# Feed-forward scales: a row of 256 values through DRAM in place of a product on TensorE

## The reference, cut to what matters

```
y = x * rsqrt(mean(x * x) + eps)          # one scale per token
x = x + s * (silu((y * g) @ w_gate) * ((y * g) @ w_up)) @ w_down     # s is 0.5 or 1.0
```

## Time and profile before

| what | value |
|---|---|
| median of 3 runs | 1790.29 us (1788.45 to 1790.33) |
| the profiled execution, its own time | 1788.07 us |
| its span in the trace | 1786.4 us |
| TensorE, weight loads, VectorE, ScalarE, GpSimd busy | 99%, 83%, 69%, 55%, 13% |
| TensorE's granted clock | 1.00 |
| mean DMA rate | 177 GB/s |

### The profile page before, as it was taken

One profiled execution on the slowest core, in us unless ns is written; L12 is line 12 of the kernel. 1 busy time (PEld: TensorE's weight loads), 2 busy tenths in 40 slices (PEclk: granted clock), 3 DMA queues, 4 the chain that ended last, 5 costly groups with the idle time before them and its releaser, 6 DMA issues.

```text
span 1786.4 us, 25450 instructions
## 1 busy us (share of the span) xinstructions
PE 1773.3 (99%) x9448; PEld 1479.0 (83%) x9448; DVE 1231.7 (69%) x1753; ACT 988.0 (55%) x1333; POOL 226.2 (13%) x255
## 2 busy tenths in 40 slices
PE   9999999999999999999999999999999999999999
PEld 8888877888888888877888877778888877788887
DVE  6775667677557755767776489976775599867763
ACT  6554586565445554666555476555554466645551
POOL 0000131000000000320000096200001383100000
PEclk9999999999999999999999999999999999999999
DMA  8756472555546564544665563535656544545651
GB/s 266 221 195 203 138 211 73 188 188 188 212 145 195 194 224 143 190 119 143 195 197 198 166 212 124 181 128 182 201 195 207 168 162 143 188 159 173 192 202 75
DMA packets 221517, 316.26 MB, mean 177 GB/s; under 512 B 14168, under 2 KB 162288, under 8 KB 221168
## 3 DMA queue, kind: packets, MB, share of 16 engines
q1 hardware_dynamic: 221392, 315.02, 54.1%
q10 hardware_dynamic: 32, 0.01, 0.0%
HBM read 313.94 MB, written 1.05 MB: 176 GB/s over the span
## 4 chain that ended last, share of the span: by engine, by line
PE 84%; DVE 9%; DVEq 3%; ACT 2%; issue 1%; ACTq 0%; POOL 0%; POOLq 0%
PE ps L2091 25%; PE ps L1955 14%; PE ps L1957 13%; PE ps L1956 13%; PE ps L2092 13%; DVE w_lo L1222 3%; PE ps L1965 1%; ACT w_hi L717 1%; PE ps L2206 1%; PE ps L2179 1%; DVEq L1706 1%; PE ps L2194 1%; DVEq L1742 1%; DVE score L1731 1%; DVE att L1755 1%
## 5 line engine op out<-in xcount | busy, mean ns | idle before, releaser
L1222 DVE TENSOR_TENSOR w_lo<-raw,w_hi 128x2048 fp32r<-128x2048 f32 (+2 forms) x296 | 674.5, 2301 | 200.9 <-ACT w_hi L717 199.2
L2091 PE MATMUL ps<-aT,w_hi 128*128 128x512 f32 x1920 | 667.9, 392 | 0.0
L717 ACT ACTIVATE w_hi<-raw 128x2048 fp32r<-128x2048 f32 (+2 forms) x296 | 551.5, 1891 | 158.9 <-PE ps L1957 155.7
L2092 PE MATMUL ps<-aT,w_lo 128*128 128x256 f32 x1920 | 537.7, 280 | 0.0
L2091 PEld LDWEIGHTS ps<-aT,w_hi 128*128 128x128 f32 x1920 | 359.2, 187 | 79.8 <-issue 0.3
L2092 PEld LDWEIGHTS ps<-aT,w_lo 128*128 128x128 f32 x1920 | 362.9, 189 | 0.2
L1955 PE MATMUL ps<-w_hi,aT 128*128 128x512 f32 (+2 forms) x768 | 309.3, 403 | 4.3 <-DVE w_lo L1222 2.8
L1957 PE MATMUL ps<-w_hi,aT 128*128 128x512 f32 (+2 forms) x768 | 295.1, 384 | 0.0
L1956 PE MATMUL ps<-w_lo,aT 128*128 128x512 f32 (+2 forms) x768 | 294.2, 383 | 0.0
L1955 PE MATMUL ps<-w_hi,gT_hi 128*128 128x512 f32 x528 | 206.0, 390 | 0.0
L1957 PE MATMUL ps<-w_hi,gT_lo 128*128 128x512 f32 x528 | 205.6, 389 | 0.0
(11 more groups left out here) (289 smaller groups left out, 1704.0 us busy)
## 6 DMA issues: line engine op xcount, KB each, us to landing
raw<-in_w_in SPq DMA_DIRECT2D x120, 512.0 KB, 4.6
raw<-in_w_ffn_down SPq DMA_DIRECT2D x88, 512.0 KB, 4.4
raw<-in_w_ffn_in SPq DMA_DIRECT2D x88, 512.0 KB, 5.0
raw<-in_w_ffn_gate SPq DMA_DIRECT2D x86, 512.0 KB, 4.1
raw<-in_w_ffn_up SPq DMA_DIRECT2D x86, 512.0 KB, 5.1
raw<-in_w_ffn_out SPq DMA_DIRECT2D x44, 512.0 KB, 4.7
raw<-in_w_out SPq DMA_DIRECT2D x32, 512.0 KB, 4.7
raw<-in_w_ck SPq DMA_DIRECT2D x8, 512.0 KB, 3.9
```

What stands on the lines that cost most here:

```text
L717: nc.scalar.activation(dst, src, ACT.Copy).then_inc(units_hi, 1)
L1222: V.tensor_tensor(o, a, h, ALU.subtract).then_inc(units_split, 1)
L2091: M(o, wh, aT[:, :, k, :], start=k == 0, stop=False, skip_group_check=True)
L2092: r = M(o[:, 0], wl, aT_hi[:, k, :], start=False, stop=k == KC - 1, skip_group_check=True)
```

## The change

The row of scales no longer comes from TensorE. After the square root and the reciprocal, ScalarE's queue writes the 256 scales to a scratch in DRAM (one element per descriptor, since `rstd` holds one value per partition and column), waits until they have landed, and issues a second transfer that reads the 1 KB back twice into each of the 128 partitions. Only then does ScalarE go on to the silu of tile 0. VectorE waits for the second transfer where it waited for TensorE and copied. The diagonals, the product with ones, the two copies, and the `ones` tile with its fill on GpSimd are gone.

```diff
@@ allocations
-        ones = sb("ones", [P, P])
-        rstd_diag = att[:, 2048:2304]
+        scale_rows = nc.dram_tensor("scale_rows", (3 * DEPTH, SEQ), F32, kind="Internal").ap()
@@ gpsimd
-            nc.gpsimd.memset(ones[:, :], 1.0)
@@ scalar, ffn
                 def first_tile():
                     root(N)
+                    act.dma_start(scale_rows[F].rearrange("(i p) -> p i", p=P), rstd[:, 0:2],
+                                  allow_slow_non_contiguous=True).then_inc(row_written, 16)
+                    act.wait_ge(row_written, (F + 1) * 16)
+                    act.dma_start(rstd_row.rearrange("p (c n) -> p c n", c=2),
+                                  scale_rows[F:F + 1, :].unsqueeze(1).broadcast_to([P, 2, SEQ])).then_inc(row_loaded, 16)
                     act.wait_ge(units_used, st.used(p0 + 1))
@@ vector, ffn
                     if isinstance(t, int) and t == 1:
-                        dve.wait_ge(row_T, F + 1)
-                        V.tensor_copy(rstd_row[:, 0:SEQ], ps[:, 4, 0:SEQ])
-                        V.tensor_copy(rstd_row[:, SEQ:2 * SEQ], ps[:, 4, 0:SEQ])
+                        dve.wait_ge(row_loaded, (F + 1) * 16)
...
                     norm(N)
-                    for i in range(2):
-                        o = V.tensor_scalar(rstd_diag[:, P * i:P * i + P], ident[:, :], rstd[:, i:i + 1], None, ALU.mult)
-                    o.then_inc(diag_ready, 1)
@@ tensor, ffn
                 turned_tile(1, p0 + 2)
-                pe.wait_ge(diag_ready, F + 1)
-                M(ps[:, 4, 0:SEQ], ones[:, :], rstd_diag, start=True, stop=True).then_inc(row_T, 1)
```

More of the change, by code:

```diff
@@ L261, in build @@
         up_lo = sem("up_lo")
-        diag_ready = sem("diag_ready")
-        row_T = sem("row_T")
+        row_written = sem("row_written")
+        row_loaded = sem("row_loaded")
         gate_scaled = sem("gate_scaled")
```

## The result

The changed kernel takes 1826.74 us (median of 6 runs, 1824.92 to 1834.14) against 1788.49 us for the kernel before beside it (1788.10 to 1790.33): ratio 1.0217, 95% interval 1.0206 to 1.0227. The prediction was 1790.8 us, 0.86 on no change and 1788.0 to 1794.5 as its range: it was wrong. Span against span it is 1825.5 - 1786.4 = 39.1 us more.

The account below looks back on a forecast made before the run. The prediction took TensorE's stream as the bound. Removing the product gains 2.6 us and a stall in the first feed-forward loses 3.1: +0.5 us on the median 1790.29 gives 1790.8 us, range 1788.0 to 1794.5.

Parts of the forecast that it names:

- L: Time from issue to landing of ScalarE's write of the scales; taken as 3.5 us, with 2.0 as lower bound.
- upper bound: Longest landing allowed for the scales' write: 8.0 us, from a weight load close by in the first feed-forward.
- a stop costs no more than its length: TensorE's stall at tile 2 was counted only as its standing time: 2.9 us plus 0.15 in the first feed-forward.
- The mechanism of the wait: ScalarE's wait delays silu and splits: 4.1 us in the first feed-forward; 2.7 in the others, hidden up to L = 6.0.
- Rival (b): TensorE stops in all six feed-forwards, from L = 6.0 on; at 8.0, +15 us, 1805 us; chance 0.04.
- +2.5: Upper end in us, like -1.0 below, to which the range added about a microsecond for the spread of runs.
- All stops together: TensorE stands at tile 2 in the first feed-forward only, 3.1 us lost; the other five hide their delay.
- The product's 0.43 us a feed-forward: Removing TensorE's product with ones moves transposes and tile 2 up by 0.43 us, 2.6 us over six feed-forwards.
- Rival (d): Handover between tile 1 and transposes fills the gap, so TensorE gains nothing; first feed-forward loses 2.7, 1793.0 us; chance 0.05.
- Rival (e): TensorE's clock falls to half rate after the stop, losing 1.8 us: +2.3, 1792.6 us; chance 0.05.
- SyncE's later loads: Loads of the next units leave later when splits free slots late; 4.1 us in the first feed-forward reach no one.
- The read: The 256 KB read back arrives before VectorE asks, at 37.3 against 38.2 us in the first feed-forward; costs nothing.

Follow-up runs that it names:

- e2: Changed kernel, but the write is two rows of 512 bytes from the identity matrix instead of the scales; 1791.83 us, ratio 1.0021.
- e6: Kernel before without diagonals, product and copies, nothing in their place; tiles 1 to 10 are multiplied by values of `x`; 1787.95 us, ratio 0.9990.
- e12: Changed kernel, but the 256 single elements are written 64 bytes apart and the row is read from an input; 1792.31 us, one run.
- e4: Changed kernel with spare transposes into an unused bank where TensorE would stand, 48 and 20 in the first feed-forward, 5 and 20 in the others; 1823.93 us, ratio 1.0204.
- e11: Changed kernel with TensorE's wait for tile 2's unit moved ahead of the transposes and filled with 60 or 25 spare transposes; 1819.44 us, ratio 1.0169.
- e7: Changed kernel, but ScalarE waits for the write and issues the read only after silu and both splits; VectorE waits at the row's use; 1799.67 us, ratio 1.0062.
- e8: Changed kernel with both transfers issued from GpSimd's queue, so ScalarE never waits and VectorE waits at the row's use; 1809.99 us, ratio 1.0120.
- e1: Changed kernel, but the same 1 KB is written as 128 runs of 8 bytes, in another order of tokens; 1796.2 us, one run.
- e3: Changed kernel, but the 256 single elements are written 512 bytes apart and the row is read from an input; 1797.0 us, one run.
- e9: Changed kernel, but the first feed-forward keeps the product; the other five write 8-byte runs and VectorE reads with matching stride; 1788.44 us, ratio 0.9996.
- e5: Kernel before, product kept, with only the write of the scales and ScalarE's wait for it added; 1810.01 us, ratio 1.0114.
- e13_late_9: Kernel before with nine extra copies on ScalarE behind the square root of each of the last five feed-forwards, no transfer; 1818.88 us, one run.
- e13_late_11: Kernel before with eleven extra copies on ScalarE behind the square root of each of the last five feed-forwards, no transfer; 1829.51 us, ratio 1.0219.
- e10: Changed kernel with TensorE's wait for tile 2's first unit moved ahead of the transposes, without spare transposes; 1827.71 us, ratio 1.0218.

## Why the prediction was wrong

**The step that failed is the size of L.** It was taken as 3.5 us, with 8.0 as its upper bound; it measured 8.7 to 10.0. The number came from three nearest rows, and the nearest in shape, 256 single elements, is a *read* from DRAM, 5.0 us. A write of adjacent single elements had no row. e2 shows in its profiled run that with an L near the assumed one the stops and the product come out: F0 +2.28 against a forecast of 3.1 - 0.43 = +2.7, the others -0.40 to -0.47 against -0.43, the span within 0.3 us of before. Its median, 3.6 us above before, shows that a forecast without the clock would have been too low even then. The upper bound was wrong for the same reason: it was read from loads that stand in line, as if waiting were the only thing that could make a transfer slow.

The Trainium skill ("DMA: Bandwidth & Descriptors", section "Latency and other measured facts") puts the fixed cost of a small transfer at about 2 us. e2, with 2.6 to 3.1 us from write to read, is near it; the changed kernel's 9.4 is more than four times as much.

**A second step failed with it: that a stop costs no more than its length.** With the measured L the prediction's own sum is -2.6 + 8.9 + 5 x 3.4 = +23 us. The rest of the 39.1 are two terms that its sum put at nothing, the clock (a rival of its own) and the pace, worked out below.

**The mechanism of the wait was right, and so was its arithmetic.** With L = 9.3 put into the prediction's own formulas: the table load comes at 26.23 + 9.3 = 35.53 in F0, and 0.22 later since the whole start is; it came at 35.83. In the sixth, with L = 8.7, it is late by 8.7 - 0.79 = 7.9; from square root to table load it took 1652.48 - 1642.97 = 9.51 against 1611.32 - 1609.71 = 1.61, so 7.90. The sixth's stop then is 7.9 - 5.2 = 2.7 us; 2.56 were measured. In F0 it is 31.85 + 9.9 - 33.02 = 8.7; measured is 7.97 us of idle time, with the transposes at half rate between its two parts. Rival (b), all six wait, is what happened; I gave it 0.04, and priced it at +15 with L = 8.0 and without the clock. A slip in the range changes nothing: a microsecond beyond "+2.5" is 1793.8, not 1794.5, and the +2.5 itself has no term in the sum, whose upper end is +2.0.

**All stops together: predicted 3.1, measured 23.9 us**, as above.

**The product's 0.43 us a feed-forward: right.** 0.43 to 0.47 in three of the last five of e6, and 0.41 to 0.49 in e12. That is -2.7 us. Rival (d) is refuted.

**The clock: right in kind, wrong in place.** Rival (e) gave 1.8 us for one fall, worked out from the earlier trace rows. A fall costs 1.7 us here (3.4 us of products at half rate). But I had it as a rival of its own with 0.05, once, when it is a consequence of a stop and came here with each of the six: 5 x 1.7 + 2.0 = 10.5 us. The Trainium skill ("TensorE: Matmul & The Clock Gate", section "Why this matters for your kernels") warns of gaps between bursts; the traces agree, with their dose as above. In the filled kernels e4 and e11 the cause of the stops is in place and the clock stays at 1.00.

**The pace: not seen.** The earlier trace rows has one mean for 1920 products, and I took the 347 ns for a property of the instruction. It is one of two values, and the slow one came in three feed-forwards: 3 x 1.75 = 5.2 us.

**The account.** Idle 23.9, product -2.7, clock 10.5, pace 5.2, start 0.2: 37.1 of 39.1 us; 2.0 are left over. The same prices give e4 from the changed kernel: -10.5 for the clock, three more feed-forwards at the slow pace, +5.2, so -5.3; the spans differ by 1821.4 - 1825.5 = -4.1.

**What waits else: half right.** SyncE's later loads reached nobody, as predicted. The read was costed at nothing, which holds in the changed kernel (5.4 to 6.0 us), because all that it could delay was late already; e7 and e8 show the read as the last link.

**What stays open.** Why the pace has two values, and what deals them. In the seven kernels in which the splits of F1 to F5 came in time (before, e1, e2, e3, e6, e9, e12) it was always 347 ns, 35 of 35; in the other eleven it was 353 in 34 of 55. One of these, F2 of e7, had no wait in the view of waits: two distances between starts at tile 3's beginning are 400 and 447 ns, and the pace changes there from 347 to 353. In F0 the slow one came in 8 of 18 kernels, in e6 and e9 without a wait that the trace shows. Why equal stops of 2.68 us drop the clock once and not the next time, no run here shows. That 64 bytes are the unit in which the writes collide is bounded by e1 and e12 alone; 16 and 32 bytes apart weren't tried.

The falls of the clock near 1030 to 1052 us, far from any edit, are stops too. VectorE's and TensorE's rows of e6, at the start of the attention:

```profile
1027.60 4.46 DVE L1222 TENSOR_TENSOR w_lo<-raw,w_hi 128x2048 fp32r<-128x2048 f32 x1 [0.68 <-ACT w_hi L717]
```
```profile
1032.11 0.55 PE L1950 MATMUL ps<-w_hi,aT 128*128 128x512 f32 x1 [2.31 <-DVE w_lo L1222]
```

In before this split takes 2.48 us, and TensorE waits 0.41. The long one came in six of the 18 profiled runs (e3, e5, e6, e11, e13_late_9, e13_late_11), each time with a wait of 2.3 to 2.4 us, and the clock fell behind it in three (e3, e5, e6). Why the split is slow in some runs is open.

## What to carry to other kernels

Before a small transfer is put into an engine's path, look at how closely its small writes lie in DRAM, and price it from a row of that very shape; if there is none, leave the upper bound open. Price a stop of the bounding engine as stop plus clock: here a stop of 2.6 us with the clock's fall behind it cost 4.3, and no stop of 1.7 us or less had one. And when a queue must wait, look for what stands behind it: here a wait for 1 KB held up splits of weights that had nothing to do with it.

## What the runs showed of the hardware

- A DMA write of 1 KB from 128 partitions to DRAM, issue to landing: 256 adjacent elements of 4 bytes 7.4 to 10.0 us in the kernels in which ScalarE waits for it (up to 10.5 in e7); 128 adjacent runs of 8 bytes 4.4 to 6.2; 256 elements 64 or 512 bytes apart 3.4 to 5.4; two rows of 512 bytes about 2.6 to 3.1 to the next issue.
- The same pair of transfers on GpSimd's queue: 10.1 to 11.0 us for the write and 7.7 for the read (ScalarE's: 9.4 and 5.8 in the changed kernel, 8.1 to 10.5 and 8.0 to 8.7 in e7), and 0.72 to 0.86 us of the engine for each issue.
- TensorE's products of this kernel run at one of two paces at the same granted clock, 347 and 353 ns a pair, nearly always kept until the stream is next interrupted; an interruption of 0.25 us can change it. The slow one costs 1.75 us in a feed-forward.
- Around the stops of the feed-forwards and the wait near 1050 us, where no spare work filled them, the granted clock fell to 0.50 each time with 3.0 us or more of idle time up to the end of the stop (for 3.4 us, 6.8 with some of the longer ones, 10.2 with the 9.1 us of e10's F0), in 9 of 15 cases with 2.3 to 2.7 us, and never with 1.7 us or less.
